# Most of the modulation of a two-block transformer moved from TensorE to VectorE multiply-adds

## The reference

```
mod_x = silu(c)     @ w_ada[i] + b_ada[i]      # 1024 -> 6*1024, for x
mod_c = silu(c_ctx) @ w_ada[i] + b_ada[i]      # the same weights, for the context
sh1, sc1, ga1, sh2, sc2, ga2 = split(mod_x, 6)
hx  = rms_norm(x, g1) * (1 + sc1) + sh1        # then attention and other mixers
x   = x + ga1 * mix(hx)
fx  = rms_norm(x, g2) * (1 + sc2) + sh2
x   = x + ga2 * ffn(fx)                         # layers 0, 1: silu(gate) * up; 2, 3: relu squared
```

## Time and profile before

| | |
|---|---|
| median of 3 runs | 2356.52 us |
| profiled execution, its own time | 2360.01 us |
| its span, first to last instruction | 2358.2 us |
| PE busy | 2293.3 us (97%) |
| DVE busy | 1363.0 us (58%) |
| ACT busy | 1076.3 us (46%) |
| mean granted clock of TensorE | 0.991 |

### The profile page before, as it was taken

How to read it: one execution, slowest core, us unless ns; L and a number is a source line. 1 busy time by engine, 2 the same in 40 slices (tenths; PEclk the granted TensorE clock), 3 DMA queues, 4 the chain that set the end, 5 groups by cost and what they waited for, 6 DMA issues and landing times.

```text
span 2358.2 us, 36051 instructions
## 1 busy us (share of the span) xinstructions
PE 2293.3 (97%) x14146; PEld 1882.8 (80%) x14146; DVE 1363.0 (58%) x2477; ACT 1076.3 (46%) x2066; POOL 33.4 (1%) x40
## 2 busy tenths in 40 slices
PE   8999999999889999999999999999999999999999
PEld 6658877877857999877777788888888887798888
DVE  5454433333656767577886435534434789757776
ACT  4453422223545555545557323522323765655543
POOL 0300000000100000000000000000000000000000
PEclk9999999999899999999999999999999999999999
DMA  8572333333265655355564322223222222154554
GB/s 316 183 275 97 107 109 124 116 125 107 108 228 184 196 180 171 97 188 198 208 210 152 111 96 87 83 98 99 99 91 97 90 90 77 59 171 143 196 181 141
DMA packets 95319, 335.51 MB, mean 142 GB/s; under 512 B 10672, under 2 KB 12848, under 8 KB 95024
## 3 DMA queue, kind: packets, MB, share of 16 engines
q1 hardware_dynamic: 95152, 333.21, 42.3%
HBM read 332.12 MB, written 1.05 MB: 141 GB/s over the span
## 4 chain that ended last, share of the span: by engine, by line
PE 87%; DVE 6%; ACT 5%; issue 2%; DMA 1%; SPq 0%; ACTq 0%; DVEq 0%
PE out L1433 20%; PE out L1434 19%; PE out L1435 19%; PE out L1427 7%; PE out L1431 3%; PE sc L1499 2%; DVE w_lo L1835 2%; PE pt L1508 1%; PE out L1371 1%; PE pv L1526 1%; PE pt L1371 1%; PE pv L1524 1%; PE aux L1331 1%; ACT w_hi L1565 1%; DMA raw<-stream 1%
## 5 line engine op out<-in xcount | busy, mean ns | idle before, releaser
L1433 PE MATMUL out<-act,w_lo 128*128 128x512 f32 (+1 forms) x1816 | 647.7, 357 | 8.8 <-DVE w_lo L1835 2.9
L1565 ACT CAST w_hi<-raw 128x1024 fp32r<-128x1024 f32 (+2 forms) x444 | 452.9, 1023 | 408.5 <-PE out L1435 336.8
L1434 PE MATMUL out<-act,w_hi 128*128 128x512 f32 (+1 forms) x1816 | 637.5, 351 | 0.0
L1435 PE MATMUL out<-act,w_hi 128*128 128x512 f32 (+1 forms) x1816 | 637.3, 351 | 0.0
L1835 DVE TENSOR_TENSOR w_lo<-raw,w_hi 128x1024 fp32r<-128x1024 f32 (+2 forms) x444 | 528.0, 1192 | 125.3 <-ACT w_hi L1565 124.9
L1433 PEld LDWEIGHTS out<-act,w_lo 128*128 128x128 f32 x1816 | 346.1, 191 | 64.5 <-issue 12.9
L1435 PEld LDWEIGHTS out<-act,w_hi 128*128 128x128 f32 x1816 | 345.8, 190 | 45.4
L1434 PEld LDWEIGHTS out<-act,w_hi 128*128 128x128 f32 x1816 | 346.2, 191 | 42.8
L1433 PE MATMUL out<-mix,w_lo 128*128 128x512 f32 (+1 forms) x734 | 261.2, 356 | 1.0 <-DVE mix L2144 1.0
L1434 PE MATMUL out<-mix,w_hi 128*128 128x512 f32 (+1 forms) x734 | 260.1, 354 | 0.0
L1435 PE MATMUL out<-mix,w_hi 128*128 128x512 f32 (+1 forms) x734 | 260.0, 354 | 0.0
(11 more groups left out here) (275 smaller groups left out, 2862.4 us busy)
## 6 DMA issues: line engine op xcount, KB each, us to landing
raw<-stream SPq DMA_DIRECT2D x604, 512.0 KB, 3.8
raw<-stream SPq DMA_DIRECT2D x16, 384.0 KB, 3.3
raw<-stream SPq DMA_DIRECT2D x16, 256.0 KB, 2.8
x<-xin SPq DMA_DIRECT2D x4, 512.0 KB, 5.3
consts<-const SPq DMA_DIRECT2D x1, 1088.0 KB, 7.1
x<-ctx SPq DMA_DIRECT2D x1, 1024.0 KB, 6.0
out<-x SPq DMA_DIRECT2D x8, 128.0 KB, 1.7
vecs<-vec SPq DMA_DIRECT2D x1, 287.0 KB, 9.1
```

Of the source, the lines that this page charges most:

```text
L1433: nc.tensor.matmul(ps, wl, xh, start=(k == 0), stop=False)
L1434: nc.tensor.matmul(ps, wh, xl, start=False, stop=False)
L1435: ins = nc.tensor.matmul(ps, wh, xh, start=False, stop=(k == s.nk - 1))
L1565: nc.scalar.copy(w_hi[:, number % HL, 0:n], raw[:, place[number] % RAW, 0:n]).then_inc(S["hi_ready"], 1)
```

## The change

64 units stay on PE: layer 0 banks 1 and 2, now the only ones in the attention of layer 0 (one pump fewer for each item, 3 in place of 4), and layer 2 banks 1 and 2 in the attention of layer 1, where other units stood in the same places. The other 112 become products on DVE: for each unit and each conditioning column that is needed, DVE multiplies the 128 by 1024 unit by the column's scalar of each partition and adds it to an accumulator in SBUF (mod_acc, in the stage buffer). After eight units PE sums the accumulator over its 128 partitions with four matmuls whose weights are ones, or a row of pick that steers the sum to row 0 or 1 of the quarter (a step modsum), and DVE finishes the bank as before (a step mod). 64 units (layer 1, and layer 2 bank 0) are spread over the ffn of layer 0 and give 96 products, 48 (layer 3) over the ffn of layer 2 and give 64: two columns are needed in layer 2 and in bank 0, one otherwise. The attention of layer 2 has no unit left.

```
+    def mod_sums(layer, banks):
...
+        for bank in banks:
+            conds = 2 if layer % 2 == 0 or bank == 0 else 1
+            for half in range(2):
+                for k in range(KD):
+                    unit = []
+                    for cond in range(conds):
+                        fills.append(product(unit, layer, bank, half, k, cond, conds))
+                        late = [(n - 1, f) for n, f in late]
+                        if late and late[0][0] <= 0:
+                            fills.append(late.pop(0)[1])
+                late.append((5, total(layer, bank, half, conds)))
+                if half:
+                    late.append((9, finish(layer, bank)))
...
-    seam = layer_first(0, ada_list(0, [1, 2]) + ada_list(1, [0]), 4, r)
-    seam = ffn(0, NT, [lambda a=a: ada(*a) for a in ada_list(1, [1])], seam)
-    seam = layer_first(1, ada_list(1, [2]) + ada_list(2, [0]), 3, seam=seam)
+    seam = layer_first(0, ada_list(0, [1, 2]), 3, r)
+    seam = ffn(0, NT, mod_sums(1, [0, 1, 2]) + mod_sums(2, [0]), seam)
+    seam = layer_first(1, ada_list(2, [1, 2]), 3, seam=seam)
     seam = ffn(1, NX, [], seam)
-    seam = layer_second(2, seam, ada_list(2, [1, 2]) + ada_list(3))
-    seam = ffn(2, NT, [], seam)
+    seam = layer_second(2, seam)
+    seam = ffn(2, NT, mod_sums(3, [0, 1, 2]), seam)
...
+                elif s.kind == "modsum":                      # on TensorE
+                    wait(pe, s.ready)
+                    wait(pe, s.sc_free)
+                    for cond in range(s.total):
+                        u = mod_acc[:, s.half, cond, :].rearrange("p (m q j) -> p q m j", q=4, j=32)
+                        one = ones[:, 0:2] if s.total == 1 else pick[:, 1 - cond:3 - cond]
+                        for q in range(4):
+                            ins = nc.tensor.matmul(scb[0][32 * q:32 * q + 2, s.half * NX:(s.half + 1) * NX], one, u[:, q],
+                                                   start=(cond == 0), stop=(cond == s.total - 1))
+                    ins.then_inc(S["mods_summed"], 1)
...
+                elif s.kind == "product":                     # on VectorE
+                    acc = mod_acc[:, s.half, s.which, :]
+                    unit = raw[:, s.unit.r % RAW, :]
+                    cond = cv[:, s.layer // 2, s.k, s.which:s.which + 1]
+                    dve.wait_ge(S["silu_ready"], 1)
+                    wait_landed(dve, s.unit.r)
+                    if s.k == 0:
+                        wait(dve, s.free)
+                        nc.vector.tensor_scalar(acc, unit, cond, None, ALU.mult).then_inc(S["product_added"], 1)
+                    else:
+                        wait(dve, s.before)
+                        nc.vector.scalar_tensor_tensor(out=acc, in0=unit, scalar=cond, in1=acc, op0=ALU.mult, op1=ALU.add)\
+                            .then_inc(S["product_added"], 1)
```

More of the change, by code:

```diff
@@ L59, in __init__ @@
                  blocks=None, place=None, total=None, psum=None, sq=None, r=None, made=None,
-                 ox=None, todo=None):
+                 ox=None, todo=None, used=None):
         self.kind, self.i, self.number, self.layer, self.src, self.k0 = kind, i, number, layer, src, k0
@@ L68, in __init__ @@
         self.c0, self.keys, self.steps, self.units, self.blocks, self.place = c0, keys, steps, units, blocks, place
-        self.todo = todo
+        self.todo, self.used = todo, used
         self.quarters, self.folded = {}, False
@@ L363, in ada_quarter, with product, go, total @@
         return s
+    def mod_sums(layer, banks):
+        fills, late = [], []
+        buffers = {}
+        def product(unit, layer, bank, half, k, cond, conds):
+            def go():
+                s = step("product", layer=layer, bank=bank, half=half, k=k, which=cond)
+                if cond == 0:
+                    unit.append(s)
+                    raw.append(("ada", s))
+                s.unit = unit[0]
+                s.free = last.get(("acc", half)) if k == 0 else None
+                s.before = buffers.get((half, cond))
+                buffers[half, cond] = s.done = signal("product_added")
+                if cond == conds - 1:
+                    unit[0].used = s.done
+            return go
+        def total(layer, bank, half, conds):
+            def go():
+                s = step("modsum", layer=layer, bank=bank, half=half, total=conds, ready=buffers[half, conds - 1])
+                s.sc_free = last.get(("sc", 0)) if half == 0 else None
+                last["acc", half] = s.done = signal("mods_summed")
+            return go
+        def finish(layer, bank):
+            def go():
+                s = step("mod", layer=layer, bank=bank, psum="sc", used=last["acc", 1])
+                s.mods = last["sc", 0] = signal("mods_read")
+                signal("mods_ready")
+            return go
+        for bank in banks:
[11 more added lines that the diff above has]
+                    late.append((9, finish(layer, bank)))
+        for n in range(12):
+            late = [(n - 1, f) for n, f in late]
+            fills.append(late.pop(0)[1] if late and late[0][0] <= 0 else lambda: None)
+        assert not late
+        return fills
     out_slots = 2
@@ L1101, in plan @@
                 stream.append(extra.pop(0))
-        elif s.kind in ("ada", "adq"):
+        elif s.kind in ("ada", "adq") or s.kind == "product" and s.unit is s:
             s.r = sum(1 for e in stream if e[0] != "ctx2")
@@ L1151, in build @@
         eps = sb("eps", [P, 2])
+        pick = sb("pick", [P, 3])
         rq = sb("rq", [P, 2, 8])
@@ L1224, in build @@
                    v_t[:, 0, :, :].rearrange("p t n -> p (t n)")]
-        ada_turn = stage[:, 4336:4848]
+        mod_acc = stage[:, 1088:5184].rearrange("p (h c n) -> p h c n", h=2, c=2)
         ada_banks = {"sc": scb[0], "pt": ptb[1], "out": outb[1]}
@@ L1238, in build @@
             o_mean o_guess ox_ready ox_hi ln_sum ln_sq ln_x ln_h s_done ln_done vec_in cond_in lam_in const_in ctx2_in small_in stored part_mods
-            silu_ready sin_ready turn_ready dve_seq act_seq pool_seq bank_zero lam_ready sum_exp q_guess q_norm conv_ready""".split()
+            silu_ready sin_ready turn_ready dve_seq act_seq pool_seq bank_zero lam_ready sum_exp q_guess q_norm conv_ready
+            product_added mods_summed""".split()
         S = {n: ctx.enter_context(nc.semaphore(n)) for n in names}
@@ L1284, in _ @@
                     else:
-                        sp.wait_ge(S["ada_used"], before[1].used[1])
+                        wait(sp, before[1].used)
                 n = UNIT if kind == "ada" else blocks[what][3] * P
@@ L1863, in _ @@
             nc.vector.memset(eps[:, 0:1], EPS)
+            nc.vector.memset(pick[:, 0:3:2], 0.0)
+            nc.vector.memset(pick[:, 1:2], 1.0)
             nc.vector.memset(eps[:, 1:2], HD * EPS).then_inc(S["bank_zero"], 1)
@@ L1896, in _ @@
                         nc.vector.tensor_copy(mods[:, 0, 0:1, 0:1], mods[:, 0, 0:1, 0:1]).then_inc(S["mods_ready"], 1)
+                elif s.kind == "product":
[11 more added lines that the diff above has]
+                            .then_inc(S["product_added"], 1)
                 elif s.kind == "ada":
                     split_due()
-                if s.kind == "ada" and (s.half, s.k) == (1, KD - 1):
-                    dve.wait_ge(S["ada_used"], s.used[1])
-                    tr = ada_turn if s.psum == "pt" else k_t[:, 1, :]
+                if s.kind == "mod" or s.kind == "ada" and (s.half, s.k) == (1, KD - 1):
+                    wait(dve, s.used)
+                    tr = k_t[:, 1, :]
                     nc.vector.transpose(tr, ada_banks[s.psum][:, :]).then_inc(S["mods_read"], 1)
```

## The result

The changed kernel takes 2342.4 us as the median of 4 runs (2341.0 to 2344.2), the kernel before 2356.7 us (4 runs, 2355.6 to 2357.7): a ratio of 0.994 with a 95% interval of 0.9923 to 0.9957. Five more runs of it gave 2342.5 us (0.9937, 0.9924 to 0.9951). The forecast was 2342. The total is right, but its largest term is right by two errors that nearly cancel, and three others miss by 1.5 to 4.3 us; the rest of this text takes them apart.

What follows compares the result with a forecast made beforehand. PE bounds the kernel, with DVE close behind in layer 2's heads. Terms -14.0 - 5.1 - 1.1 + 5.3 = -14.9 us from 2360.01 give 2345.1, less 3.5 for the median, 2342; range 2320 to 2352, the forecast's own 2332 to 2349.

Steps and rivals of the forecast that it cites:

- Attention of layer 2: 80 units go, 39.5 us of PE; DVE's queue leaves 37% of that as gain: -14.0 us.
- My gaps lie between the two: Layer 2's heads: expected PE gaps of 1.4 us lie between idles of 2.77 us (clock 0.71) and 0.8 us (1.00).
- Attention of layer 0: 48 units become 32; 7.0 us of PE saved, the last item's 1.9 giving nothing: -5.1 us, bounds 0 and -7.0.
- Ffn of layer 0: 16 singles go (-8.8 us), eight modsums come (+6.1), a wait at one group end (+1.6): together -1.1 us.
- The first group's end: Layer 0's ffn: three products ahead of the last hidden tile's low part delay the first down block, +1.6 us.
- A unit and a modsum: Price on PE: 0.55 us for a unit or one-column modsum, 0.97 us for a pair or two-column modsum.
- Products, room on VectorE, transfers: Layer 0's ffn: 1.22 us a product, DVE busy about 220 of 309 us, transfers at 276 GB/s cost nothing.
- rival C: Layer 0's ffn: the five-buffer ring waits for DVE's products and becomes stream-bound, +28 us, 2370 us; chance 0.06.
- Ffn of layer 2: Modsums +4.1 us, products before the last low part at three group ends +1.2 us: together +5.3 us.
- Layer 1: Its attention keeps 32 units in the same places, so nothing moves there: 0 us.
- Rival A: Whole kernel: PE is the bound everywhere and the units' whole price is paid back, -45.1 us, 2311 us; chance 0.10.
- B: Rival: layer 2 gives nothing back because PE's gaps drop its clock to 1.2 GHz in each head, 2355.6 us; chance 0.12.

Runs made afterwards that it cites:

- run 2: Changed kernel with four convolution taps ahead of the split that waits for ACT in layer 2's first seven heads, in place of two behind it: 2328.7 us.
- run 5: Kernel before, units and all, with four convolution taps moved ahead of the split that waits for ACT in seven heads of layer 2: 2354.9 us.
- run 1: Changed kernel with one to three spare matmuls on TensorE ahead of layer 2's transpositions T that had waited 0.8 us or more: 2340.0 us.
- run 8: Changed kernel once more, unchanged, timed and profiled a second time: 2342.5 us.
- run 3: Changed kernel with no product between a hidden group's last up block and the first down block, those products following one block later: 2338.4 us.

## Why the prediction was right, step by step

**Attention of layer 2: right in sum, by two errors.** The mechanism was right: DVE's queue is late next (runs 2, 5), T waits 0.8 to 1.6 us in the later items, the wait for w_hi stays at 10.9 us. The forecast gave DVE 127.7 us for the four heads; without falls of the clock they take 125.7 (run 1, 1091.21 to 1216.91), and the whole stage gives 19.5 us, not 14.0: half of the price, not 37%. The falls, to which the forecast's sum gave nothing, took 5.8 us back in the first profile and 2.1 in run 8, so that the agreement of 14.0 with 13.6 is in part chance. "My gaps lie between the two", it said of the clock's rows; the result lay between too, falls in three heads of eight. That DVE would no longer wait for PE's spread rows was right where the clock does not fall: 2.0 us are left of 3.9, both waits in heads whose clock had fallen just before, and run 1 has none in these heads.

**Attention of layer 0**: -5.1 against -4.4, right within its bounds.

**Ffn of layer 0: term by term.** The first group's end cost 1.6 us at the place and by the three products that were named (run 3). A unit and a modsum were priced too low. The 0.55 and 0.97 us of the earlier trace rows run from one start to the next instruction's start; between dense blocks the neighbours lose time too. A modsum of two columns:

```profile
1556.37 0.39 PE L1500 MATMUL out<-act,w_hi 128*128 128x512 f32 x1
1556.69 1.04 PE L1436 MATMUL sc<-stage,pick 128*2 128x256 f32 x16
1557.66 0.50 PE L1498 MATMUL out<-act,w_lo 128*128 128x512 f32 x1
1558.00 0.39 PE L1499 MATMUL out<-act,w_hi 128*128 128x512 f32 x1
```

From the matmul ahead to the modsum pass 0.32 us, from the one behind to the next 0.34, where 0.23 is the rule: 0.97 + 0.09 + 0.11 = 1.17, and the lead in the comparison of the traces falls by 1.20 at such a step, and by 0.77 at one of a single column or a unit. 16 units at 0.77 against eight modsums (four at 0.77, four at 1.20) and 1.6 us make -2.8; measured -2.6.

**Products, room on VectorE, transfers (rival C): right.** Three products take 3.6 us, from 318.83 to the 322.42 of what follows in run 3's fence, 1.20 each; 1.22 was assumed. In the stretch that answers to the earlier trace rows VectorE is busy 209 of 300 us, and the densest one moved 266 GB/s with TensorE busy throughout, at full clock:

```profile
255.00:555.00 300.00, 298.56 (x1379) 241.51 (x1378) 208.82 (x226) 76.26 (x92) 0.00 (x0) 1.00 0.59 203
341.00:434.00 93.00, 93.00 (x436) 74.48 (x435) 68.75 (x76) 24.51 (x29) 0.00 (x0) 1.00 0.78 266
```

**Ffn of layer 2: too small.** +5.3 was forecast; modsums at the right price are 5.5 in place of 4.1, the group ends 1.65 in place of 1.2, and 1.7 us is a fall of the clock at the seam into the ffn, after a wait of 1.98 us. The kernel before has the same wait, 1.98 us, at 1497.30, and its clock did not fall there; nor did it in run 8, whose ffn of layer 2 is 1.6 us shorter (588.0 against 589.6 from layer 2's last maximum to layer 3's first).

**Layer 1: not forecast.** 3.2 of its 4.3 us come at one place. A unit there waited 2.30 us for its transfer before, and the clock then stood at 0.50 (662.70 to 665.70); after the change it waits 0.53 us, and the clock stays:

```profile
662.54 1.02 PE L1371 MATMUL out<-raw,cv 128*2 128x256 f32 x8 [2.30 <-DMA raw<-stream]
...
655.32 0.61 PE L1425 MATMUL out<-raw,cv 128*2 128x256 f32 x8 [0.53 <-DMA raw<-stream]
...
655.50:658.50 3.00, 2.93 (x27) 0.92 (x20) 0.92 (x3) 0.57 (x2) 0.00 (x0) 1.00 1.02 406
```

That is no gain of the change, or not for certain: when the same kernel was profiled again (run 8) the unit waited 2.06 us once more, and layer 1 from its first maximum to its last took 1.5 us longer. What sets this transfer's time was not tried. The other 1.1 us lie at the seam into layer 1, where the clock stood at 0.50 from 635.30 to 642.10 before and at 0.75 in the matching stretch, 628.40 to 635.20, after; that the clock is their cause was not tested.

Rival A fell: T waits. Of B a part came true: the falls took some of the gain. The forecast's own range starts 1.6 us too low for its reason, since layer 2 giving 22 us makes 2333.6 and not 2332. The errors of the stages, +0.4, +0.7, -1.5, -4.3, +0.4 and +3.5 us, add up to -0.8: the cause was right, and the closeness of the total was luck as well.

## What to carry to other kernels

When work leaves the busiest engine, price it by what the next engine leaves, per stage: here 39.5 us of TensorE gave half at best, and much of the rest came only when VectorE's queue was put in another order. Then look at the stage that takes the work in: the same move cost an ffn of 512 tokens little but its modsums, and one of 256 tokens 54 us. Where products fill gaps, keep them off the places where the next matmul reads what VectorE makes last.

## What the runs showed of the hardware

The granted clock's falls are not bound to a wait's length alone. Waits of 1.3 to 1.6 us in layer 2 were followed by 1.2 GHz in some heads and not in others; one of 2.25 us was so in one profile of the same program and not in another, and a seam's 1.98 us in one profile and not in two others. Such a fall behind a wait of T made a head 0.1 to 1.5 us longer. A unit of four matmuls between dense blocks costs 0.77 us, where its own starts show 0.55.
